# Half-width first attention block, and the last pair of modulation rows moved behind the output product

## The reference, cut to what matters

```python
for l in range(DEPTH):                       # DEPTH = 2
    h = x @ w_in[l]
    ...
    proj = jnp.einsum('bsnc,ncd->bsnd', branches, w_o_branch[l])
    gates = jax.nn.sigmoid(merge.reshape(B, S, N_BRANCH, D) + b_gate[l])
    merged = jnp.sum(gates * proj, axis=2)
    out = merged @ w_out[l]
    x = _layer_norm(DEEPNORM_ALPHA * x + out, ln_g[l], ln_b[l])
```

```python
s = jnp.einsum('bqhd,bkhd->bhqk', q_blk, k).astype(jnp.float32) * scale
s = jnp.where(key_idx[None, :] <= q_idx[:, None], s, MASK_VALUE)   # MASK_VALUE = -1e30
pr = jax.nn.softmax(s, axis=-1).astype(v.dtype)
```

## Time and profile before

| | us |
|---|---|
| median of three executions | 2873.32 |
| profiled execution | 2875.91 |
| its span | 2874.0 |
| TensorE (PE) busy | 2751.8 (96%) |
| GpSimd (POOL) busy | 1342.9 (47%) |
| VectorE (DVE) busy | 1017.6 (35%) |
| ScalarE (ACT) busy | 659.9 (23%) |
| mean granted TensorE clock | 0.985 |

### The profile page before, as it was taken

One profiled execution on the slowest core, in us unless ns is written; L12 is line 12 of the kernel. 1 busy time (PEld: TensorE's weight loads), 2 busy tenths in 40 slices (PEclk: granted clock), 3 DMA queues, 4 the chain that ended last, 5 costly groups with the idle time before them and its releaser, 6 DMA issues.

```text
span 2874.0 us, 44404 instructions
## 1 busy us (share of the span) xinstructions
PE 2751.8 (96%) x17617; PEld 2292.7 (80%) x17617; DVE 1017.6 (35%) x1586; ACT 659.9 (23%) x1220; POOL 1342.9 (47%) x608
## 2 busy tenths in 40 slices
PE   8999999999999997999999999999999999898998
PEld 7987778689777775888878778888888888776996
DVE  1752653247428333001341533002330023524237
ACT  3432212144222122000131443001130001415101
POOL 4830000077000002666655555666655656667786
PEclk9999999999999998999999999999999999999999
DMA  6556643445565343322222122222223222232443
GB/s 226 187 186 231 248 168 128 186 168 180 201 260 223 149 171 108 118 89 101 100 91 99 49 55 102 101 99 92 102 88 102 88 102 91 100 117 73 148 167 140
DMA packets 68318, 390.25 MB, mean 136 GB/s; under 512 B 19184, under 2 KB 20816, under 8 KB 21968
## 3 DMA queue, kind: packets, MB, share of 16 engines
q1 hardware_dynamic: 66336, 379.03, 36.9%
q10 hardware_dynamic: 1840, 9.18, 0.9%
HBM read 387.09 MB, written 1.10 MB: 135 GB/s over the span
## 4 chain that ended last, share of the span: by engine, by line
issue 25%; POOL 11%; POOLq 10%; PE 9%; DMA 3%; DVE 1%; SPq 1%; ACT 0%; DVEq 0%; ACTq 0%
POOL m_ws L1718 9%; POOLq L1717 7%; DMA m_ring<-in_panels 3%; PE m_bank L1884 2%; POOLq L1730 1%; PE m_bank L1801 1%; POOL m_ws L1736 1%; PE m_bank L1802 1%; PE m_bank L1803 1%; POOLq L1735 1%; PE m_bank L2017 1%; SPq L1674 1%; PE m_bank L2029 1%; PE m_bank L1980 1%; PE m_bank L1982 1%
## 5 line engine op out<-in xcount | busy, mean ns | idle before, releaser
L1801 PE MATMUL m_bank<-m_aT,m_ws 128*128 128x512 f32 (+1 forms) x1792 | 632.1, 353 | 34.9 <-DVE m_aT_low L2379 15.6
L1803 PE MATMUL m_bank<-m_aT,m_ws 128*128 128x512 f32 (+1 forms) x1792 | 628.5, 351 | 0.0
L1802 PE MATMUL m_bank<-m_aT_low,m_ws 128*128 128x512 f32 (+1 forms) x1792 | 628.4, 351 | 0.0
L1718 POOL TENSOR_TENSOR m_ws<-m_ring,m_ws 128x2048 fp32r<-128x2048 f32 x127 | 593.5, 4673 | 18.7
L1884 PE MATMUL m_bank<-m_ws,m_hs 128*128 128x512 f32 x1848 | 422.6, 390 | 3.5 <-DVE m_ws L2416 1.4
L1801 PEld LDWEIGHTS m_bank<-m_aT,m_ws 128*128 128x128 f32 x1792 | 345.7, 193 | 82.8 <-issue 23.7
L1884 PEld LDWEIGHTS m_bank<-m_ws,m_hs 128*128 128x128 f32 x1848 | 346.1, 188 | 79.3 <-issue 6.9
L371 POOL TENSOR_TENSOR m_ws<-m_ring,m_ws 128x2048 fp32r<-128x2048 f32 x48 | 221.6, 4627 | 345.9 <-ACT m_ws L886 345.9
L1802 PEld LDWEIGHTS m_bank<-m_aT_low,m_ws 128*128 128x128 f32 x1792 | 345.8, 193 | 42.3
L1803 PEld LDWEIGHTS m_bank<-m_aT,m_ws 128*128 128x128 f32 x1792 | 345.3, 193 | 42.1
L2422 DVE TENSOR_TENSOR m_hidT<-m_sg,m_bank 128x512 f32 (+3 forms) x88 | 54.6, 621 | 688.9 <-ACT m_sg L2189 688.9
(11 more groups left out here) (348 smaller groups left out, 3428.7 us busy)
## 6 DMA issues: line engine op xcount, KB each, us to landing
m_ring<-in_panels SPq DMA_DIRECT2D x352, 1024.0 KB, 4.9
m_rows<-m_gg_dram ACTq DMA_DIRECT2D x6, 1024.0 KB, 5.4
m_bias<-in_rpb SPq DMA_DIRECT2D x48, 64.0 KB, 2.7
m_hT<-in_ln_rows ACTq DMA_DIRECT2D x2, 1024.0 KB, 7.1
m_con<-in_con SPq DMA_DIRECT2D x1, 1536.0 KB, 10.4
memT_ctx<-in_memT SPq DMA_DIRECT2D x1, 1024.0 KB, 5.7
x_tok<-in_x SPq DMA_DIRECT2D x1, 1024.0 KB, 13.9
memT_ctx<-in_ctx SPq DMA_DIRECT2D x1, 1024.0 KB, 6.9
```

The source lines that it names most:

```text
L1718: nc.gpsimd.tensor_tensor(ws[:, p, 1, :], ring[:, p, :], ws[:, p, 0, :].bitcast(F32), ALU.subtract)\
L1801: mm(out, w, a, start=start, stop=False)
L1802: mm(out, w, a_low, start=False, stop=False)
L1803: return mm(out, w_low, a, start=False, stop=stop)
```

## The change: what it does, and the diff

It does two things.

*First attention block.* For `a` = 0 only the first 128 keys are taken: the 8 score matmuls have 128 columns instead of 256; DVE's masking, maxima and scaling, ScalarE's exponentials and its copies of the transposed probabilities have half the elements; there are 8 transposes instead of 16, and 8 matmuls with the values instead of 16. The masked half is not computed at all.

*Modulation pairs 7 and 8.* Pair 7 (rows and columns) stood in the second half of the scan (`i` = 1), between its first products. Now nothing stands there. It takes the place of pair 8, around `gate(1, 0)` and `gate(1, 1)` behind the scan. Pair 8 now stands at the very end of the layer, behind the four `out` panels, and on ScalarE behind the square root of the layer norm. The order of the panels in memory and in the ring follows, and the layer norm waits for the use of panel `("out", 3)` instead of the last panel.

```diff
@@ stream_of_a_layer
     columns_of(6)
+    gate(0, 1)
+
     rows(7, 0)
+    gate(1, 0)
     rows(7, 1)
-    columns_of(7)
-    gate(0, 1)
-
-    rows(8, 0)
-    gate(1, 0)
-    rows(8, 1)
     again()
     gate(1, 1)
-    columns_of(8)
+    columns_of(7)
     branch(0)
     branch(1)
     feeds(*[("out", n) for n in range(4)])
+    rows(8, 0)
+    rows(8, 1)
+    columns_of(8)
@@ TensorE, attention
                     nh = 8 if a < 2 else 4
+                    keys = P if a == 0 else T
                     for h in range(nh):
-                        out = A(h // 2)[:, (h % 2) * T:(h % 2 + 1) * T]
+                        out = A(h // 2)[:, (h % 2) * T:(h % 2) * T + keys]
                         if a < 2:
-                            last = mm(out, qf[0:96, h, i * P:(i + 1) * P], kf[0:96, h, :], start=True, stop=True)
+                            last = mm(out, qf[0:96, h, i * P:(i + 1) * P], kf[0:96, h, 0:keys], start=True, stop=True)
...
                     for h in range(nh):
-                        for kt in range(2):
+                        for kt in range(keys // P):
                             last = transpose(A(h // 2)[:, ((h % 2) * 2 + kt) * P:((h % 2) * 2 + kt + 1) * P],
...
-                        for kt in range(2):
+                        for kt in range(keys // P):
                             if a < 2:
...
-                                          start=(kt == 0), stop=(kt == 1))
+                                          start=(kt == 0), stop=(kt == keys // P - 1))
@@ TensorE, scan
                         if g == 1 and i == 0:
                             gate(7, 1)
-                        elif g == 1:
-                            mod_rows(7, 0)
-                            mod_rows(7, 1)
                         elif g == 3 and i == 0:
                             mod_rows(6, 0)
                             mod_rows(6, 1)
-                        elif g == 3:
-                            mod_columns(7)
@@ TensorE, behind the scan
-                mod_rows(8, 0)
+                mod_rows(7, 0)
                 gate(1, 0)
-                mod_rows(8, 1)
+                mod_rows(7, 1)
...
                 gate(1, 1)
-                mod_columns(8)
+                mod_columns(7)
                 pe.wait_ge(s["rw_done"], l + 1)
                 branch(0)
                 branch(1)
...
                     last.then_inc(s["panel_used"], 1)
+                mod_rows(8, 0)
+                mod_rows(8, 1)
+                mod_columns(8)
@@ ScalarE, attention
-                        src = prob[:, h * T:(h + 1) * T] if a < 2 else A(h // 2)[:, (h % 2) * T:(h % 2 + 1) * T]
-                        last = a_(prob[:, h * T:(h + 1) * T], src, ACT.Exp, bias=small[:, h:h + 1], scale=sc,
+                        at = slice(h * T, h * T + (P if a == 0 else T))
+                        src = prob[:, at] if a < 2 else A(h // 2)[:, (h % 2) * T:(h % 2 + 1) * T]
+                        last = a_(prob[:, at], src, ACT.Exp, bias=small[:, h:h + 1], scale=sc,
...
-                        last = a_(probT[:, 4 * b:4 * b + 4, :], A(b).rearrange("p (b q) -> p b q", q=P), ACT.Copy)
+                        step = 2 if a == 0 else 1
+                        last = a_(probT[:, 4 * b:4 * b + 4:step, :], A(b).rearrange("p (b q) -> p b q", q=P)[:, ::step, :], ACT.Copy)
@@ ScalarE, scan and end of the layer
                     if i == 0:
                         gate(7, 1)
-                    else:
-                        mod_rows(7)
...
                         mod_rows(6)
-                    else:
-                        mod_columns(7)
...
                 gate(1, 0)
-                mod_rows(8)
+                mod_rows(7)
...
                 gate(1, 1)
-                mod_columns(8)
+                mod_columns(7)
...
                 act.wait_ge(s["ln_var"], l + 1)
                 a_(small[:, 70:72], small[:, 68:70], ACT.Sqrt, bias=eps_ln[:, :]).then_inc(s["ln_std"], 1)
+                mod_rows(8)
+                mod_columns(8)
@@ VectorE, attention and layer norm
-                    p3 = prob[:, 0:nh * T].rearrange("p (h k) -> p h k", k=T)
+                    keys = P if a == 0 else T
+                    p3 = prob[:, 0:nh * T].rearrange("p (h k) -> p h k", k=T)[:, :, 0:keys]
...
                     else:
-                        dve.wait_ge(s["panel_used"], l * PANELS1 + PANELS1)
+                        dve.wait_ge(s["panel_used"], l * PANELS1 + PANEL[("out", 3)] + 1)
```

6 lines of the change are left out of this document (3 added, 3 removed).

## The result

The changed kernel took 2876.9 us (median of 20 runs, 2873.2 to 2880.4), the kernel before 2873.7 us beside it; the ratio is 1.0013, 95% interval 1.0007 to 1.0019. Two of the 20 executions of the kernel before took 12416.58 and 6253.08 us and are not in the ratio. So the changed kernel is 2 to 5.5 us slower, where 2.1 us less were forecast. It stays within 0.2%, the likeliest class, but 0.4 us above the range (2866.0 to 2876.5 us).

The account below looks back on a forecast made before the run. TensorE was taken to set the pace in the first part, with short exceptions. Terms -6.8 - 5.6 + 10.3 = -2.1 us took the 2873.32 us median to 2871.2 us; range 2866.0 to 2876.5 us.

Parts of the forecast that it names:

- The attention: First attention block: halved scores, transposes and value products take 3.4 us off TensorE per layer, 6.8 us for two layers.
- The scan's second half: Without pair 7 the step behind the fourth group comes 2.8 us earlier per layer, 5.6 us for two.
- Pair 7 for pair 8: Behind the scan: pair 7 takes pair 8's place with the same instructions, panels and copies; zero.
- The end of layer 1: Pair 8 hides beside the layer norm, where TensorE is idle; zero, bound 1 us.
- Rival 3: Second part starts 4.2 us late, waiting for `ctx`, issued later; sum +2.1, 2875.4 us; chance 0.06.
- rival 4: Attention's 6.8 us saving absent, as TensorE waits it elsewhere; +4.7, 2878.0 us; chance 0.06.
- rival 2: Clock falls at every lengthened wait, in layer 1's scan and fully at layer 0's end; +0.1, 2873.4 us; chance 0.12.
- Rival 1: Scan gives back 3.0 us more (clock drop, hole), layer 0's end costs only 8.5; -6.9, 2866.4 us; chance 0.20.
- the end of layer 0: Pair 8 hides behind nothing there: its work, waits, branch and half a clock drop cost 10.3 us, bounds 8.5 and 11.5.
- the same 2.49 us from the columns' start: Layer 0's end: TensorE's loop branch costs what ScalarE's hole showed, 2.49 us, so `mem` begins at about 566.4.
- The sign named in advance: Layer 0's end: `mem` starts 9 to 11 us behind the last output product.
- 1.47 us without a recorded cause: Hole in layer 1's scan, while four panels were streaming; entered as zero, with 1.5 us each way kept per layer.

Follow-up runs that it names:

- experiment 5: The kernel before plus six float32 products of constants, then TensorE waiting for its own last product ahead of the loop's branch; 2889.03 us, ratio 1.0055, five runs.
- experiment 4: The kernel before plus one TensorE wait for its own last output panel ahead of the loop's branch, no work added; 2880.77 us, ratio 1.0023.
- experiment 7: The changed kernel with pair 8's rows ahead of the fourth output panel and ScalarE's column copy ahead of its layer norm wait; 2883.26 us, 1.0029 of before.
- padded kernels: Kernels with 16 small products of constants added to each layer: with the halved attention 2869.93 or 2866.67 us by place, in the kernel before 2880.99 us.
- experiments 2: The kernel before with only pairs 7 and 8 moved as in the change, attention not halved; 2878.04 us, ratio 1.0015.
- experiment 10: The kernel before with the halved attention and 16 small products of constants in the fourth attention unit's wait; 2866.67 us, ratio 0.9968.

## Why the prediction was wrong

**Right.** The attention: -6.8 forecast, -6.4 in the changed kernel, -6.9 alone, the softmax early as said. The scan's second half: -5.6 forecast, -5.8 measured, with the last wait 1.78 us where 1.9 was named. Pair 7 for pair 8: zero. The end of layer 1: zero. Rival 3 (late `ctx`) and rival 4 (no saving) are refuted, and rival 2 in the scan: behind the lengthened wait of 1.78 us the clock stayed at 1.00 in both layers. Rival 1 was right in the scan, where both of its 1.5 us came off (more on this under luck), and furthest off at the end of layer 0, with 8.5 us. At the end of layer 0 the places of every wait: 2.32 us for the panel (2.4 forecast), 0.72 for ScalarE (0.85), then one without a cause.

**The step that failed** is the end of layer 0, 10.3 us forecast with 11.5 as its upper bound, 16.0 measured. The text took "the same 2.49 us from the columns' start" for the branch back, "because ScalarE's row is the nearest", and half of 1.5 us for the clock. TensorE stood for 5.50 us, and even with the DMA engines at rest its branch costs 3.9 (experiment 5), 4.1 in experiment 4. The nearest row was one of another engine, taken with the DMA engines less loaded, and the bound of 11.5 us left only 1.2 us over the forecast for both. The low clock cost 2.50 us and not 0.75: the 1.5 us were read from a step of 2 us of work, with the clock high again behind it; here it was low from 555.8 to 566.0, and 5 us of that fell on `mem` products. From the columns' start to `mem` it took 6.55 us (554.56 to 561.11) where I had 2.5, which is 4.0 short; with the clock's 1.75 that is the whole of the miss (16.04 - 10.3). The sign named in advance, `mem` 9 to 11 us behind the last output product, failed with it: it is 13.4 us.

**The term that was missing** is the scan's first half, +3.0 us. The instructions there are not touched; only their distance from the layer's start changed. I had one such hole in my rows, "1.47 us without a recorded cause", and entered zero for it. I put it down to the panels that "were streaming"; but the earlier trace rows ends 2 us ahead of it, and in the hole itself (1008.1 to 1009.6 us) the DMA share is 0.10. The thirteen traces of this study, with the list ahead from 32 products longer to 24 shorter, put the first hole behind 2719 to 2721 recorded products of the layer each time, while its place in the dense run moved with the padding, from 71 to 125. The other holes of over 0.3 us stand behind 2842, 2962, 3587 and 3831 (give or take 3), 123 apart or about a multiple of it; the 1.47 us of the earlier trace rows are one behind 3587. Which of these places shows a hole differs from kernel to kernel, and in part from layer to layer.

The Trainium skill ("Runtime: NRT & Kernel Launch", Instruction fetch mechanics) has instructions fetched in blocks of 256, and calls the cost of crossing one mostly hidden. 123 products with as many weight loads, and the few register instructions between, are about one such block, so the trace agrees with the block. It does not agree with "mostly hidden" in a run of 64x64 products at 31 ns each: the first hole is 1.2 to 2.8 us long, beside a DMA share of 0.8 to 1.0, and the later ones reach 2.4 us; those of them that stand at a share of 0.00 still take 0.3 to 1.6 us. That the holes are fetches is the reading that fits their places; no row of a trace names a fetch.

**Luck.** The steps behind the second half's products gave -2.04 us in layer 1 where I had zero, for the hole of 1.47 is gone with pair 7. In layer 0 they gave -2.17, of which 1.5 us is the fall of the clock that was there in the trace before and not in the one after; of the five traces without pair 7 in the scan, only that of experiment 7 has it in layer 0. Entered together, and without that 1.5 us, the unforeseen terms are +3.0 and -2.7 in the scan and +5.7 at the layer's end; the last decides. The forecast's sign would have been right only without it.

**Open.** What decides whether a given place shows a hole, and how long it gets, with the same instructions ahead of it too; why the second halves pay in the padded kernels; whether a loaded DMA, or the two engines' branching together, accounts for 5.50 against 3.91; why the `in` products run 1% slower in some layers.

## What to carry to other kernels

An engine's queue of long work hides a loop's branch only as long as nothing behind it waits: do not put a wait for a late event, with little work behind it, last in a loop body. Price a new place for a piece of work by the queue of the engine that does it, not by the other engines' idle time: beside a layer norm TensorE had none to give in layer 0, and all it needed in layer 1. A price borrowed from another engine is a guess about its size: here the borrowed 2.49 us was 5.50. In a long loop body 16 matrix instructions more or fewer can change holes in dense runs hundreds of us later by some us: compare the untouched pieces of two traces too, and try the same edit with padding before judging a gain of 0.1%.

## What the runs showed of the hardware

- A loop's branch back with a dry queue: TensorE 3.91 us at a DMA share of 0.02, 4.08 at 0.57, 4.84 at 0.98, 5.50 at 1.01; ScalarE 2.3 to 2.6 at 0.2 to 0.3, 5.11 and 5.26 at about 1. With products queued ahead: none seen (0.36 us, for a bank).
- In the four us behind these holes TensorE's granted clock was 0.50 (changed kernel, experiments 2 and 4) and 0.59 (experiment 5). It did not fall at one point of them: in the changed kernel it fell as the columns ended, ahead of the hole, in experiment 4 within it, in experiment 5 at its end.
- Steps of 1.7 us from single falls of the clock come and go between executions in pieces with the same instructions. So do steps of 0.7 us, from `in` products that run 1% slower at a granted clock of 1.00.
- Holes in dense runs of 64x64 products keep their places by the count of recorded products of the layer (2719, 2842, 2962, 3587, 3831), and come at DMA shares of 1.01 and of 0.00.
- 32 recorded 64x64 products of constants took 2.07 us in experiment 10, 65 ns each, twice the 31 ns of the dense runs.
